# Three units of gate products moved out of the start of the sparse attention stage

## What is computed

```python
h = rmsnorm(x, norm_mix)
(a_b, a_c, a_x, qb, kb, vb, qc, kc, vc, qi, ki, wi, g_a, g_b, g_c) = jnp.split(h @ w_in, SPLIT_POINTS, axis=-1)
...
o_c = dsa_prompt(qc, kc, vc, qi, ki, wi)      # per 128 queries: top 256 keys by indexer score, then attention
br_c = o_c @ w_dsa_o
merged = jax.nn.sigmoid(g_a) * br_a + jax.nn.sigmoid(g_b) * br_b + jax.nn.sigmoid(g_c) * br_c
x = x + merged @ w_out
```

## Time and profile before

| | |
|---|---|
| median of 3 runs | 1817.97 us (1817.0 to 1820.09) |
| the profiled execution: time, span | 1821.46 us, 1819.7 us |
| mean granted clock of PE | 0.989 |
| busy: PE, DVE, ACT, POOL | 97%, 70%, 40%, 32% |
| sparse stage (first filler unit to the last) | 717.2 to 950.5 us |

### The profile page before, as it was taken

How to read it: one execution, slowest core, us unless ns; L and a number is a source line. 1 busy time by engine, 2 the same in 40 slices (tenths; PEclk the granted TensorE clock), 3 DMA queues, 4 the chain that set the end, 5 groups by cost and what they waited for, 6 DMA issues and landing times.

```text
span 1819.7 us, 32206 instructions
## 1 busy us (share of the span) xinstructions
PE 1758.0 (97%) x12267; PEld 1705.2 (94%) x12267; DVE 1277.8 (70%) x2222; ACT 727.0 (40%) x1273; POOL 588.1 (32%) x477
## 2 busy tenths in 40 slices
PE   4999999999999999898989999999999999999998
PEld 4999999989999998777889999999999999999998
DVE  6256869969878867688957347876666666776765
ACT  4233112348821132777762425333333333422334
POOL 2111212237643333422232000565555555121030
PEclk7999999999999999999999999999999999999998
DMA  4111111110111213311122311222222222542212
GB/s 151 35 35 35 47 30 50 49 39 24 35 48 35 58 27 82 82 42 35 51 59 62 130 46 35 83 83 83 72 82 83 83 71 74 191 130 81 93 36 96
DMA packets 180436, 121.22 MB, mean 67 GB/s; under 512 B 9340, under 2 KB 165260, under 8 KB 180300
## 3 DMA queue, kind: packets, MB, share of 16 engines
q1 hardware_dynamic: 179324, 117.37, 21.4%
q0 software_dynamic: 976, 2.00, 0.4%
HBM read 101.45 MB, written 17.89 MB: 66 GB/s over the span
## 4 chain that ended last, share of the span: by engine, by line
PE 86%; DVE 7%; ACT 2%; issue 2%; POOL 1%; DMA 1%; SPq 0%; DVEq 0%; ACTq 0%; POOLq 0%
PE ps L1329 37%; PE ps L1681 22%; PE ps L1754 7%; PE ps L1740 6%; PE ps L1438 3%; PE ps L1341 3%; PE ps L1461 3%; PE ps L1576 2%; PE ps L1536 2%; DVE probs L2736 1%; DVE key_mask L2551 1%; DVE top L2551 1%; ACT probs L2057 0%; DMA x_rows<-in_x_prompt 0%; DMA w_raw_in_lo<-in_w_in 0%
## 5 line engine op out<-in xcount | busy, mean ns | idle before, releaser
L1075 POOL TENSOR_TENSOR w_lo<-w_raw,w_hi 128x1024 fp32r<-128x1024 f32 (+1 forms) x53 | 100.6, 1898 | 354.6 <-ACT w_hi L1842 354.6
L1329 PE MATMUL ps<-h_hi,w_hi 128*128 128x352 f32 (+1 forms) x936 | 206.4, 329 | 3.9 <-POOL w_lo L1075 3.9
L1329 PE MATMUL ps<-h_hi,w_lo 128*128 128x352 f32 (+1 forms) x936 | 203.2, 325 | 0.0
L1329 PE MATMUL ps<-h_lo,w_hi 128*128 128x352 f32 (+1 forms) x936 | 202.8, 325 | 0.0
L2551 DVE MAX8 top<-key_mask 128x8 f32<-128x768 f32 (+5 forms) x192 | 170.4, 889 | 11.8 <-PE ps L1329 1.2
L2551 DVE MATCH_REPLACE8 key_mask<-top,key_mask 128x768 f32<-128x768 f32 (+5 forms) x192 | 167.7, 876 | 0.9 <-issue 0.9
L1329 PEld LDWEIGHTS ps<-h_hi,w_hi 128*128 128x128 f32 (+1 forms) x936 | 158.9, 189 | 6.6 <-issue 4.9
L1329 PEld LDWEIGHTS ps<-h_hi,w_lo 128*128 128x128 f32 (+1 forms) x936 | 161.1, 188 | 0.5
L1329 PEld LDWEIGHTS ps<-h_lo,w_hi 128*128 128x128 f32 (+1 forms) x936 | 159.5, 188 | 0.5
L1681 PE MATMUL ps<-mix_hi,quarter_hi 128*128 128x264 f32 x672 | 136.9, 285 | 0.3 <-ACT x_one L1842 0.3
L1681 PE MATMUL ps<-mix_hi,quarter_lo 128*128 128x264 f32 x672 | 136.4, 284 | 0.0
(11 more groups left out here) (357 smaller groups left out, 4549.8 us busy)
## 6 DMA issues: line engine op xcount, KB each, us to landing
w_raw_in_lo<-in_w_in SPq DMA_DIRECT2D x56, 256.0 KB, 2.8
w_raw<-in_w_in SPq DMA_DIRECT2D x54, 256.0 KB, 3.0
ffn_tiles<-t SPq DMA_DIRECT2D x44, 264.0 KB, 2.4
w_raw<-in_w_gate SPq DMA_DIRECT2D x44, 256.0 KB, 3.1
w_raw<-in_w_up SPq DMA_DIRECT2D x44, 256.0 KB, 3.1
w_raw<-in_w_down SPq DMA_DIRECT2D x32, 192.0 KB, 2.7
w_raw_in_lo<-in_w_in SPq DMA_DIRECT2D x44, 128.0 KB, 2.2
ffn<-ffn_tiles SPq DMA_DIRECT2D x20, 264.0 KB, 4.4
```

The lines of the kernel that those rows point to most:

```text
L1075: nc.gpsimd.tensor_tensor(WLO[:, k, 0:tiles, :], raw[:, k, 0:tiles, :], WHI[:, k, 0:tiles, :].bitcast(F32), ALU.subtract).then_inc(lo_read ...
L1329: last = nc.tensor.matmul(PS[0:rows, NB * k + b, 0:e - a], w[:, k, t, 0:rows], x[:, t, a:e], start=m == 0 and w is WHI and x is hi, stop=m ...
```

## The change

The second fixed place has no units any more. The rest of `sparse_slots` is as it was, so the three units are dealt out over the places behind.

```diff
-FIRST_SLOTS = {(-1, 0): KT, (-1, 1): 3}
+FIRST_SLOTS = {(-1, 0): KT, (-1, 1): 0}
```

## The result

The changed kernel takes 1823.32 us (median of 8 runs, 1821.7 to 1825.15) where the kernel before takes 1818.32 us (8 runs, 1815.88 to 1820.09). The ratio is 1.0028, with a 95% interval of 1.0020 to 1.0037: slower by 5.1 us (3.6 to 6.7). The forecast was 1.3 us faster, and the range ended at 1820.0.

A forecast was written before the change was run, and what follows sets the result against it. PE, busy 97% of the span, was taken to bound the kernel. Terms of +0.2, -0.4, -0.8 and -0.3 us sum to -1.3, taking 1817.97 to 1816.7 us; the range was 1814.2 to 1820.0.

The forecast's parts named there:

- start, idle time: Start of the stage: PE's wait for the weights' low part moves to other operations, 3.3 us instead of 3.12, +0.2 us.
- start, clock: Start of the stage: PE's clock still falls, but less busy time runs at the low level, cost 2.4 instead of 2.8, -0.4 us.
- single-unit turns, idle time: Turns 1, 4 and 7 instead of 2, 5 and 8: PE's waits 3.7 us against 4.5, -0.8 us.
- behind tile 1, idle time: From turn 9 on: chain ahead, units lagging into tiles 4 and 5 where PE is often idle, -0.3 us (-0.7 to +0.7).
- Slower: the single-unit turns get worse: Turns 3 and 6: ACT waiting for a load delays masks of turns 4 and 7 by 1.5 us each; 1820.4 us, chance 0.14.
- The clock does not fall: Start of the stage: scores of pair 2 break the idle time, PE's clock stays up; 1814.5 us, chance 0.12.
- The lead is swallowed: Late turns: lagging units pay back the start's gain; between -0.5 and +0.5 us, 1818.0 us, chance 0.26.

The follow-up runs named there:

- x5: Changed kernel with the splits of the later weight halves of jobs 4 and 6 put one turn later on ACT and POOL; -0.4 us against the kernel before.
- x4: Kernel before with only the start changed: no units behind the first two scores, six instead of three at turn 0's first place; -1.6 us against before.
- x3: Changed kernel with 36 added products, results unread, filling PE's waits around turns 4 and 7; +2.2 us against the kernel before.
- x2: Kernel before up to turn 8, with the changed kernel's unit counts from turn 9 on; +3.1 us against the kernel before.
- x11: Changed kernel with only the split of job 4's later weight half moved from turn 3 to turn 4; +2.9 us against the kernel before.
- x6: Kernel before with 27 added products, results unread, in PE's 3.12 us wait between the first two scores and the first unit; -3.1 us against before.
- x1: Changed kernel's unit counts up to turn 8, counts of the kernel before from turn 9 on; +4.4 us against the kernel before.
- x10: Changed kernel with three units put back behind the first scores and one left at turn 0's second place; +5.5 us against the kernel before.
- x7: Kernel before with turn pairs (1, 2), (4, 5), (7, 8) holding four and four units instead of seven and one; -0.5 us against before.
- x8: x1 with the later-half splits of jobs 4 and 6 moved one turn later, as in x5; -1.5 us against the kernel before.
- x9: Kernel before with x4's empty start, x7's four-and-four turns and added products in PE's turn 0 waits; -2.0 us against before.

## Why the prediction was wrong, point by point

Set side by side, the four terms of the forecast and what the profiles show for them:

| term | forecast | measured |
|---|---|---|
| start, idle time | +0.2 | 2.89 - 3.12 = -0.2 |
| start, clock | -0.4 | 2.4 - 2.8 = -0.4 |
| single-unit turns, idle time | -0.8 | 4.47 - 4.47 = 0.0 |
| behind tile 1, idle time | -0.3 | +2.1 |
| clock behind turns 4 and 7 | no term | +4.4 (by x5) to +4.8 |

The measured column adds up to 5.9 to 6.3 us; the stage is 5.4 us longer in the profiles, the kernel 5.1 us slower.

**Start, idle time: right within half a microsecond.** The forecast had +0.2 us, measured are 0.78 + 2.11 = 2.89 against 3.12 us. The moved wait, its place and its cause (one DVE instruction of 1.88 us beside POOL's subtraction, in both profiles) are as told.

**Start, clock: right.** The fall is there, and cheaper by 0.4 us, as forecast. Run by itself, x4 shows the start at -1.6 us (-3.3 to -0.2), more than the -0.2 us that these two terms forecast together and the -0.6 that the profile shows for them.

**The single-unit turns: this is the step that failed.** Two things in it were wrong. The first is the wait. It was put as -0.8 us, with 1.4 us of waiting in turn 4 and 1.9 in turn 7. Measured are 2.41 and 2.06, 4.47 us together, the sum of before. Turn 7 is nearly as forecast. In turn 4 ACT stood 2.14 us at the split of a later half, where the forecast had no delay of that kind. The prediction took this wait to be alike in both kernels, one turn ahead of the single-unit turn. It is not: in the kernel before ACT waits 0.8 us for a load in turn 1, not at all in turn 4 and 1.5 us in turn 7; in the changed kernel 2.1 us in turn 3 and not at all in turn 6.

The second is larger, and it was put at nothing without a reason of its own: the clock behind these turns. It was asked about at the start alone, with the gaps of up to 2.0 us in the late turns as the evidence that gaps of that size leave it at 1.00. In turns 4 and 7 it fell, at a price of 4.4 to 4.8 us. x3 and x5 show that this is where most of the loss lies: without these falls 2.9 us come back, and with the two splits moved out of turns 3 and 6 all of it.

**Behind tile 1: the sign was wrong, too.** -0.3 us by the forecast. From turn 9 on PE's waits sum to 19.6 us after and 17.5 before (brackets of its timeline, 0.15 us and more): +2.1, three times the bound of 0.7. x2 has +3.1 us for these turns, with a fall of the clock in turn 15. The lagging units did not fall into free time. Why the wait of turn 15 grows from 0.57 to 1.90 us was not taken apart, and stays open.

**The rivals.** "Slower: the single-unit turns get worse" named a mechanism that x11 and x5 bear out for turn 4, ACT in its queue at the split, with the scaling behind it. It is not what happens in turn 7, and it priced only the waits, 1820.4 us. Its condition, a load "that lands more than about 1 us later" than the 3.80 us of the row, was not met: the transfer landed 3.51 us after its issue (4.19 against 4.36 us, counted from the first of the two transfers), and ACT waited all the same. The row that it was measured by was itself one of the late ones, where others take 2.2 us. "The clock does not fall" was wrong at the start (0.51 from 721.3 us on), and asked the right question in the wrong place. "The lead is swallowed" did not come about as told. The lead was there, 1.3 us at the scores of pair 5 in turn 3 (19.8 us after the start of the stage, 21.1 before), and turn 4 lost it.

## What to carry to other kernels

When fixed counts move a list of work by a few entries, compare where its boundaries fall, not how much it moves: here the same pattern of turns, one turn earlier, brought ACT to a split 2.1 us ahead of its load, where it had come 0.2 us after it. In the rows ACT's scaling, low share and exponentials all stand behind such a split; put a turn later, where the load had landed, it cost nothing that the times show (x5). Don't take one row for the time of a load: the row used here, 3.80 us, was among the slowest of a kind whose median is 2.2. And price each wait of PE twice, once as idle time and once as what its clock may do to the work behind it, most of all where a dense stretch follows.

## What the hardware showed beyond that

Whether the clock falls after a wait of about 2 us is not a matter of its length alone. Waits of 1.93 and 1.96 us in turns 5 and 8 left it up in the profile before, as 1.92 us in turn 5 did in x4, but in x6, with 1.93 us in turn 5, it fell (at 30 us). 2.4 to 2.7 us in turn 4 and 2.0 to 2.1 us in turn 7 brought it down in each of the three profiles that have both (changed, x1, x10), and 2.0 us in turn 7 in x11. But x2 has 1.65 + 0.85 = 2.50 us in turn 5 (ACT waited 1.12 us there, for a transfer of 4.1 us), and its clock stays at 1.00 from 741 to 752 us. So a fall is not certain either, and the price of a wait differs between executions. Late waits of 1.8 to 2.0 us brought it down in some profiles and not in others of the same order of work: at 89 us in x2 and x3, not in the changed kernel, x5, x10 or x11; in turn 21, at 135 to 143 us, in x1, x6, x7 and x8, not in the kernel before, x4 or x9. A single profile does not tell which of these waits a kernel pays for.

PE kept busy through its wait with products of no use gained 3.1 us in x6 and 2.9 us in x3. In x9 the same device at another place did not keep the clock up, it only shortened the stretch at the low level.

And the time of a transfer of 128 KB in this stage went with whether a packet of 16 KB of the instruction queue ran beside it: never over 2.5 us without one (449 transfers), up to 4.1 with one (97 transfers).
